# Weight products of a two-layer decoder trunk: three rounded float32r matmuls, or one float32 matmul on the loaded tile

## The reference

```python
for i in range(2):
    mod = silu(c) @ ada_w[i] + ada_b[i]                 # (2048) @ (2048, 12288): read once, a matrix-vector product
    sh1, sc1, g1, sh2, sc2, g2 = split(mod, 6)
    h = x * (1 + sc1) + sh1
    y = s5_mixer(h) if i == 0 else dsa_mixer(h)         # h @ in_w, scan, gelu, @ glu_w  |  h @ in_w, top-64 attention, @ out_w
    x = layer_norm(ALPHA * x + (1 + g1) * y)
    h = x * (1 + sc2) + sh2
    g, u = split(h @ ffn_w_in[i], 2)                    # 2048 -> 2 x 5632
    x = layer_norm(ALPHA * x + (1 + g2) * ((silu(g) * u) @ ffn_w_out[i]))
```

## Time and profile before

| | |
|---|---|
| median of 3 runs | 2871.43 us (2863.91 to 2874.15) |
| span of the profiled execution | 2871.0 us |
| TensorE busy, matmul records | 2560.3 us (89%), 12057 |
| VectorE busy | 2021.9 us (70%) |
| ScalarE busy | 1097.5 us (38%) |
| DMA | 627.74 MB, mean 219 GB/s |
| mean granted TensorE clock | 0.940 |

### The profile page before, as it was taken

The page is one execution under the profiler, slowest core; times in us unless marked ns, Lnnn a source line. Parts: engine busy times, 40 slices in busy tenths (PEclk is TensorE's granted clock), DMA queues, the critical chain, the costliest instruction groups (busy, mean ns, idle before and its releaser), DMA issues.

```text
span 2871.0 us, 35599 instructions
## 1 busy us (share of the span) xinstructions
PE 2560.3 (89%) x12057; PEld 2050.4 (71%) x12057; DVE 2021.9 (70%) x3615; ACT 1097.5 (38%) x1242; POOL 38.5 (1%) x69
## 2 busy tenths in 40 slices
PE   4369668789889999999998999987979999999996
PEld 3357234278768888888886788875868888888885
DVE  6664899958877777677766888678677755455456
ACT  0134532033344434443444344445344434443442
POOL 0000000000000000000000000000000000000000
PEclk8579989889989999999999999977999999999998
DMA  5865313468868888888874788840659856666663
GB/s 195 317 215 192 118 57 124 158 211 306 297 210 285 289 292 292 279 269 286 284 230 161 265 276 273 278 132 26 198 189 306 277 189 193 190 188 193 192 188 126
DMA packets 314890, 627.74 MB, mean 219 GB/s; under 512 B 30816, under 2 KB 31104, under 8 KB 314496
## 3 DMA queue, kind: packets, MB, share of 16 engines
q1 hardware_dynamic: 310272, 611.28, 64.3%
q0 software_dynamic: 4480, 14.68, 1.9%
HBM read 623.77 MB, written 2.10 MB: 218 GB/s over the span
## 4 chain that ended last, share of the span: by engine, by line
PE 71%; DVE 18%; DMA 5%; issue 2%; ACT 2%; SPq 1%; DVEq 0%; POOL 0%; ACTq 0%
PE psB L1495 34%; PE psA L1495 33%; DVE prod L1019 4%; DVE tmp L1024 3%; DVE st L1028 3%; DMA col_raw<-in_ada_w 2%; PE psT L1256 2%; DMA w_raw<-in_s_glu_w 1%; DVE col_acc L828 1%; DVE w_lo L790 1%; DVE ada_acc L802 1%; DMA w_raw<-in_ffn_w_in 1%; PE psM L1273 1%; ACT w_hi L575 0%; ACT st L655 0%
## 5 line engine op out<-in xcount | busy, mean ns | idle before, releaser
L790 DVE TENSOR_TENSOR w_lo<-w_raw,w_hi 128x1024 fp32r<-128x1024 f32 x776 | 947.0, 1224 | 626.9 <-ACT w_hi L575 623.0
L575 ACT ACTIVATE w_hi<-w_raw 128x1024 fp32r<-128x1024 f32 x776 | 819.9, 1060 | 1225.3 <-PE psB L1495 499.9
L1495 PE MATMUL psA<-w_hi,hT_hi 128*128 128x512 f32 (+1 forms) x1216 | 480.6, 395 | 22.4 <-DVE w_lo L790 20.7
L1495 PE MATMUL psB<-w_hi,hT_hi 128*128 128x512 f32 x1184 | 472.6, 399 | 9.0 <-DVE w_lo L790 9.0
L1495 PE MATMUL psA<-w_hi,hT_lo 128*128 128x512 f32 (+1 forms) x1216 | 476.0, 391 | 0.0
L1495 PE MATMUL psA<-w_lo,hT_hi 128*128 128x512 f32 (+1 forms) x1216 | 475.8, 391 | 0.0
L1495 PE MATMUL psB<-w_lo,hT_hi 128*128 128x512 f32 x1184 | 463.9, 392 | 0.0
L1495 PE MATMUL psB<-w_hi,hT_lo 128*128 128x512 f32 x1184 | 463.9, 392 | 0.0
L802 DVE SCALAR_TENSOR_TENSOR ada_acc<-ada_raw,csil,ada_acc 128x512 f32<-128x512 f32 x480 | 359.0, 748 | 13.0 <-DVE ada_acc L802 0.9
L1495 PEld LDWEIGHTS psA<-w_hi,hT_hi 128*128 128x128 f32 x1216 | 232.8, 191 | 72.0 <-DVE w_lo L790 20.3
L1495 PEld LDWEIGHTS psB<-w_hi,hT_hi 128*128 128x128 f32 x1184 | 223.9, 189 | 61.3 <-DVE w_lo L790 12.6
(11 more groups left out here) (272 smaller groups left out, 2314.6 us busy)
## 6 DMA issues: line engine op xcount, KB each, us to landing
w_raw<-in_ffn_w_in SPq DMA_DIRECT2D x352, 512.0 KB, 4.5
ada_raw<-in_ada_w SPq DMA_DIRECT2D x512, 256.0 KB, 4.9
w_raw<-in_ffn_w_out SPq DMA_DIRECT2D x176, 512.0 KB, 4.7
col_raw<-in_ada_w SPq DMA_DIRECT2D x128, 512.0 KB, 4.8
w_raw<-in_dsa_in_w SPq DMA_DIRECT2D x112, 512.0 KB, 4.9
w_raw<-in_s_glu_w SPq DMA_DIRECT2D x64, 512.0 KB, 5.4
w_raw<-in_s_in_w SPq DMA_DIRECT2D x32, 512.0 KB, 5.9
w_raw<-in_dsa_out_w SPq DMA_DIRECT2D x32, 512.0 KB, 4.7
```

Source lines behind the costliest of these rows:

```text
L575: nc.scalar.activation(w_hi[:, n % RING], w_raw[:, n % RING], ACT.Copy).then_inc(w_hi_ready, 1)
L790: V.tensor_tensor(w_lo[:, n % RING], w_raw[:, n % RING], w_hi[:, n % RING].bitcast(F32), ALU.subtract).then_inc(w_lo_ready, 1)
L1495: ins = MM(PS[s][:, t, 0:r.width], a_[:, kt, tok], b_[:, n % RING, kk, 0:r.width], start=kt == 0 and m == 0, stop=k == r.units - 1 and kk ...
```

## The change

The splitting goes, for weights and for activations. TensorE reads `w_raw` and one float32 tile of activations (`hT`, `aT`) and issues one float32 matmul where there were three of float32r. The rings `w_hi` and `w_lo` are no longer written by the stream; the slot of `w_raw` becomes free when TensorE has used it (`w_used`), where before it became free when VectorE had taken the remainder. TensorE waits for the load itself (`w_landed`). The scale-and-shift of ScalarE writes `hT` directly and its semaphore `T_free` lets TensorE begin; so do the gelu, the feed-forward middle and the attention output. `rows_added` is a semaphore for an addition that a removed step used to order.

```diff
-                            sp.wait_ge(w_lo_ready, u + (n - RING + 1 + early))
+                            sp.wait_ge(w_used, u + (n - RING + 1 + early))
...
-            def hi_unit(u, n):
-                act.wait_ge(w_landed[n % RING], u * (16 // RING) + (n // RING + 1) * 16)
-                if not (isinstance(u, int) and u + n < RING):
-                    act.wait_ge(w_used, u + (n - RING + 1))
-                nc.scalar.activation(w_hi[:, n % RING], w_raw[:, n % RING], ACT.Copy).then_inc(w_hi_ready, 1)
...
                     act.wait_ge(T_full, r.hturn + g + 1)
-                    if g >= 2:
-                        act.wait_ge(h_ready, r.h0 + g - 1)
-                    h32 = stg[g % 2][:].rearrange("p a (b t) -> p (a b) t", t=SEQ)
                     for j in range(4):
                         k = 4 * g + j
-                        ins = nc.scalar.activation(h32[:, j], T[:].rearrange("p a (b t) -> p (a b) t", t=SEQ)[:, j],
+                        ins = nc.scalar.activation(hT[:, k], T[:].rearrange("p a (b t) -> p (a b) t", t=SEQ)[:, j],
                                                    ACT.Identity, scale=scol[:, k:k + 1], bias=bcol[:, k:k + 1])
                     ins.then_inc(T_free, 1)
-                    act.wait_ge(T_free, r.hturn + g + 1)
-                    nc.scalar.activation(hT_hi[:, 4 * g:4 * g + 4], h32, ACT.Copy).then_inc(h_hi, 1)
...
-                nc.scalar.activation(y_act[:], y_in[:], ACT.Gelu_apprx_tanh).then_inc(g_ready, 1)
-                act.wait_ge(g_ready, ch + 1)
-                nc.scalar.activation(hT_hi[:, :, ch * TC:(ch + 1) * TC], y_act[:], ACT.Copy).then_inc(g_hi, 1)
+                nc.scalar.activation(hT[:, :, ch * TC:(ch + 1) * TC], y_in[:], ACT.Gelu_apprx_tanh).then_inc(s5_done, 1)
...
-            def lo_unit(u, n):
-                vec.wait_ge(w_hi_ready, u + (n + 1))
-                V.tensor_tensor(w_lo[:, n % RING], w_raw[:, n % RING], w_hi[:, n % RING].bitcast(F32), ALU.subtract
-                                ).then_inc(w_lo_ready, 1)
...
-                        if not (stop and n + AHEAD >= r.per):
-                            lo_unit(u, n + AHEAD)
                         if r.before == "ln" and isinstance(i, int) and i == 0 and n in (3, 6, 9, 12):
+                            vec.wait_ge(T_full, r.hturn + n // 3)
                             affine(r.norm, n // 3 - 1, ALPHA)
...
-                        pe.wait_ge(w_lo_ready, u + (n + 1))
+                        pe.wait_ge(w_landed[n % RING], u * (16 // RING) + (n // RING + 1) * 16)
...
-                                for m, (a_, b_) in enumerate(((hi, w_hi), (hi, w_lo), (lo, w_hi))):
-                                    ins = MM(PS[s][:, t, 0:r.width], a_[:, kt, tok], b_[:, n % RING, kk, 0:r.width],
-                                             start=kt == 0 and m == 0,
-                                             stop=k == r.units - 1 and kk == UK - 1 and m == 2)
+                                ins = MM(PS[s][:, t, 0:r.width], src[:, kt, tok], w_raw[:, n % RING, kk, 0:r.width],
+                                         start=kt == 0, stop=k == r.units - 1 and kk == UK - 1)
```

More of the change, by code:

```diff
@@ L27 @@
 F32 = mybir.dt.float32
-F32R = mybir.dt.float32r
 I32 = mybir.dt.int32
@@ L460, in _ @@
                 if r is glu:
-                    sp.wait_ge(w_lo_ready, glu.unit)
+                    sp.wait_ge(w_used, glu.unit)
                     layer, c0 = column_source(STAGE)
@@ L734, in turned @@
                 if r.kind == "ff" and s == 1:
[L735 removed]
+                    read_T(r, i, 0, aT[:, ds(i * 4, 4)])
                 if r.kind == "ki" and s == 0:
@@ L743, in _ @@
                     s5()
-                    act.wait_ge(y_full, SEQ // TC)
-                    act.wait_ge(g_hi, SEQ // TC)
                 elif r.before == "attention":
                     attention()
[L748 to L752, removed]
                 if r.before in ("x", "ln"):
@@ L756, in _ @@
                     u = r.unit + i * r.per
-                    stop = isinstance(i, int) and i == r.n - 1 and (r is runs[0] or r is runs[-1])
                     last = closing(r, i)
@@ L968, in make_h @@
                 make_scale(r)
-                for g in range(5):
-                    if g < 4 and r.before == "ln":
+                if r.before == "ln":
+                    for g in range(4):
                         normalise(g).then_inc(xn_ready, 1)
-                    if g >= 1:
-                        vec.wait_ge(h_hi, r.h0 + g)
-                        V.tensor_tensor(hT_lo[:, 4 * g - 4:4 * g].rearrange("p a t -> p (a t)"),
-                                        stg[(g - 1) % 2][:].rearrange("p a t -> p (a t)"),
-                                        hT_hi[:, 4 * g - 4:4 * g].rearrange("p a t -> p (a t)").bitcast(F32), ALU.subtract
-                                        ).then_inc(h_ready, 1)
             def affine(norm, chunk, scale, last=None):
@@ L1031, in s5 @@
                             post(ch - 1)
-                        if ch >= 1 and t == 36:
-                            gelu_lo(ch - 1)
                     vec.wait_ge(rec, n)
@@ L1043, in s5 @@
                     ins = V.tensor_tensor(part, part, PS[s][:, :, 0:CW // P], ALU.add)
-                link(ins)
-                gelu_lo(SEQ // TC - 1)
+                ins.then_inc(rows_added, 1)
+                vec.wait_ge(rows_added, 1)
             def rope(r, i, s, heads, half, table):
@@ L1130, in attention @@
                                         ).then_inc(p_ready, 1)
-                    if a % 4 == 3 and a >= 7:
-                        o_lo(a // 4 - 1)
-                o_lo(A // 4 - 1)
             def chain_at(r, i, s):
@@ L1193, in _ @@
                     attention()
-                if r is runs[0] or r is glu:
-                    for n in range(AHEAD):
-                        lo_unit(r.unit, n)
                 if r.before in ("x", "ln"):
@@ L1225, in _ @@
                                 store_chunk(q, q_first)
-                        if n == 3 and last:
-                            turned(*last, last[0].blocks - 1)
                         if r.kind == "glu" and n == r.units + 2:
```

61 lines of the change are left out of this document (19 added, 42 removed).

## The result

| | before | after |
|---|---|---|
| median | 2871.4 us (2863.9 to 2874.2, 4 runs) | 3354.6 us (3347.8 to 3356.7, 4 runs) |
| ratio to before, 95% interval | | 1.168 [1.166, 1.171] |
| span of the profiled execution | 2871.0 us | 3345.9 us |
| TensorE clock granted, mean | 0.940 | 0.957 |

The change makes the kernel 483 us slower. 3356 was forecast.

The account below looks back on a forecast made before the run. TensorE's matmul records times their distance were taken to bound about 2200 of 2871 us. 2871.0 + 546.8 for longer products - 62 for removed waits gave 3355.8, predicted as 3356, range 3325 to 3405.

Parts of the forecast that it names:

- The product, +546.8 us: Weight-product stream: a full unit goes from 2.720 to 3.432 us, 0.712 us more for each of 768 units.
- The gains, 62 us: Places where TensorE stood still for the splitting: 9 + 10 + 30 + 13 us taken off.
- start of "u": At the start of "u", remainders and rounding that TensorE waited for go: 9 us, bounds 3.5 and 13.
- S5 scan: The remainder of L1004 leaves VectorE's scan, 1.14 us three times: 3.4 us gained.
- end of S5 and "glu": At the end of S5 the third unit's load is freed earlier, 6.6 us; "glu" was put at nothing.
- first layer norm's block: First 16 units after the first layer norm: 56.2 us become 47; its share of the norms' 30 us is 9.1.
- attention, third layer norm: Remainders leave VectorE's queue: 8 us before attention and 5 in it, 13 together; 9.0 at the third layer norm.
- What is added: Weight loads: lead falls from up to seven units to three, 10.3 us, against a 4.5 us median load; cost put at nothing.
- The rival of late loads: In each of 32 `ada_w` chunks a load takes 12.0 us and TensorE waits 2.1: 67 us, 3423 in all; chance 0.10.
- The dear record: In the weight-product stream a float32 record takes 440 ns, not 429.1: 3424 us in all; chance 0.05.
- the lower clock: A pure float32 stream is granted less clock, 26 us for each hundredth, three of them 3435; chance 0.03.
- The case of not slower: Every weight product under 0.70 us makes the change pay; at one 0.2267 us record, loads set 2337 us; chance 0.02.

Follow-up runs that it names:

- e1_split_kept: The kernel before with all splitting and its waits kept, only the three float32r products replaced by one float32 product; 3391.3 us, ratio 1.181.
- e9_halves: The changed kernel with each product of 512 columns made as two of 256 with the same stationary tile; 3368.5 us, ratio 1.172.
- e2_three_r: The changed kernel with ScalarE's rounding of each unit put back and three float32r products, VectorE's remainders still out; 2812.8 us, ratio 0.979.
- e4_lead2: The changed kernel with weight loads at most two units ahead of use, where it was three; 3374.3 us, ratio 1.174.
- e3_one_r: The changed kernel with ScalarE's rounding put back and one float32r product, without correction; 2190.8 us, ratio 0.763.

## Why the prediction was right

**What bounds the kernel.** Right: the time was the number of records times their distance. e1_split_kept changes that product alone and has 107% of the whole loss. (The "about 2200 us" of such time was loose: 768 units of 2.720 us are 2089. The sum does not use it.)

**The product, +546.8 us.** The record was put at 0.4291 us from two rows of before; it is 0.4292, so the term becomes 0.713 x 768 = 547.6. The block of 16 units was forecast at 56.7 us and runs from 894.46 to 951.13, 56.67. The decisive step was to price the new matmul by one that already stood in the same stream and to get its digits from a row of back-to-back ones; e9_halves confirms the split into columns and a constant by halving the columns.

The Trainium skill, "FP8 and Floating Point Precision", section "TensorE Precision Notes", lists true float32 as four passes through the array. The traces agree: 858 ns are four times 213.3 and 5. The 131 ns for 512 columns, which the prediction's last rival quotes from the Trainium skill, "TensorE: Matmul & The Clock Gate", section "Back-to-back issue gap", is not seen in any of these kernels; the shortest distance measured is 215.8.

**The gains, 62 us.** By the medians they were 546.8 - 483.2 = 63.6. Between the two traces they were 74 us to the end of the last product. The table sets the prediction's terms beside the stages; "between the traces" is 0.712 us for each full unit of a stage, less what the stage became longer:

| term | predicted | between the traces |
|---|---|---|
| start of "u" | 9 | 10.4 |
| S5 scan | 3.4 | 8.1 |
| end of S5 and "glu" | 6.6 and 0 | 11.6 |
| first layer norm's block | 9.1 | 9.4 |
| layer 0's feed-forward, second layer norm | 11.9 | 13.5 |
| attention, third layer norm | 13 and 9.0 | 21.7 |
| layer 1's feed-forward | 0 | -0.5 |

The norms and attention came out to within 2 us. The excess is in two places, the scan, and the stretch from its end through "glu" (11.6 against 6.6). Of the 11.6, 8.8 were gained by the end of the first eight units, whose successors start at 625.58 before and at 626.83 after. The term counted there the wait for the third unit's load, and not what stood behind the wait in the kernel before: TensorE had been idle for 4.48 us, and its next six units took 19.17 us where 72 records take 16.32, since the granted clock was at its low level again:

```profile
606.00:610.00 4.00, 3.60 (x9) 2.83 (x10) 1.91 (x3) 1.99 (x2) 0.00 (x0) 0.50 1.04 383
```

The other 2.9 us belong to the rest of "glu", which was put at zero, its waits for the splitting set against late loads. The splitting's waits were there before: in the chain of the kernel before, rounding, remainder and the load that they held back follow each other through the second half of the run, as in these rows (start, length, work):

```profile
684.19 1.24 DVE w_lo L790
685.58 5.43 DMA w_raw<-in_s_glu_w
691.03 1.07 ACT w_hi L575
```

The late loads did not come. After the change the chain from the first product of "glu" to the last is TensorE's alone, and the 9.97 us of the earlier trace rows have no successor either:

```profile
596.35 30.48 PE psA L1416 x64
626.83 20.60 PE psB L1416 x48
...
655.15 27.47 PE psA L1416 x64
```

The scan's excess is not the change's. Its length, from the first step to the last copy of `carry`, varies between kernels that have the same steps. Without the remainder of L1004 the six traces give 262.1 (after), 262.8, 267.2, 267.2, 267.6 and 267.7 us, mean 265.8; with it the four give 267.1, 268.0, 270.3 (before) and 273.1, mean 269.6. The 3.8 us between the means fit the 3.4 that were predicted, though each group spreads over 6 us. The pair of before and after happened to lie 8 apart. The two rows that this is read from, of the changed kernel and of e9_halves (durations min/median/max, first and last start):

```profile
L975 DVE TENSOR_TENSOR st<-tmp,st x512: 200/217/779, 311.4 to 573.3; 128x64 f32<-128x64 f32 x171
...
L980 DVE COPY carry<-st x4: 226/227/227, 371.4 to 573.5; 128x128 f32<-128x128 f32 x4
```

```profile
L975 DVE TENSOR_TENSOR st<-tmp,st x512: 200/228/1903, 313.9 to 581.4; 128x64 f32<-128x64 f32 x171
...
L980 DVE COPY carry<-st x4: 226/226/227, 373.9 to 581.6; 128x128 f32<-128x128 f32 x4
```

What makes the scan's length vary stays open.

In one respect the working was too simple. It counted the longer products and the gains as if they were independent. e1_split_kept and e2_three_r show that about 23 us of stalls go with either. The sum was right because the gains were counted once, but from this working the price of one half alone (the splitting's removal in a slow stream) would have been put at 62, and it is 37.

**What was luck.** The terms and the mechanism hold, but 3356 against 3354.6 is closer than the parts are. Term by term the two traces lie 12 us over the forecast of the gains; 8.3 of that vanish in the medians, because of where the two profiled executions lay in their spreads, and 2.3 in the stretch behind the last product, which took that much longer after the change. Two slips of the working are smaller than that: the step from the span to the time was put at 0.4 us and is 1.9 in every run on record, which makes the forecast's own sum 3357.7; and the larger gains add up to 76 us by the bounds given, 14 over 62, where the range took 16.

**What is added.** The load waits were put at nothing, and in the trace they are 0.7 us over all products; the landing times fell as forecast. e4_lead2 shows what stood behind that zero: with a third less of lead it would have been 20 us. The rival of late loads at 67 us was priced with the worst landing in each chunk; in the whole chain of the changed kernel a load into `w_raw` stands once, and TensorE waits those 0.7 us for it:

```profile
2563.76 10.80 DMA w_raw<-in_ffn_w_in
```

**The other rivals.** The dear record (440 ns) and the lower clock fell with the 0.4292 us and the 1.00 in the stream. Of the signs that were named, VectorE's busy time is off, 1065 us against about 1020; the products wait for it 0.4 us in all. The case of not slower needed 0.70 us for a product and got 0.858. Its end of 2337 us, the loads' pace, was itself too high by the rate it assumed: e3_one_r, with one product of 0.2267 us, took 2191.

## What to carry to other kernels

- Price a new instruction by the same shape in the old trace, in the stream where it will stand, and by its distance from the next, not by its busy time. Here two readings of the old trace, the sum over a chunk and the back-to-back row, gave the record's length to 0.1%.
- Fewer instructions and two idle engines are worth little where the third is the bound. 1790 us of work on VectorE and ScalarE went for 37 us (59 or more at the old pace), since it stood beside TensorE.
- A stall that a change removes may also be gone by another part of the same change. Do each half alone before the gain is credited to one of them.
- A row of the chain says what was waited for, and not that the engine stood still. Read the engine's own timeline for the wait, and the granted clock behind it: at the first layer norm of e1_split_kept, 2.1 us of waiting stood in front of 2.0 us more of low clock.

## What was not expected of the hardware

- A float32r matmul of 512 columns takes 226.7 ns from start to start; a bfloat16 one 215.8, and a float32 record with two sweeps of 256 columns 215.8 too. The 11 ns are float32r's own and cost this kernel about 93 us in 2872.
- Loads of 512 KB and 256 KB from one queue reached 371 GB/s at a DMA share of 1.02, though the kernel before had 294 GB/s at 0.88.
- The same chain of small VectorE steps in the S5 scan took 262 to 268 us in six traces in which the same steps stood in it.
- Behind a short wait of TensorE the granted clock was low again: after 2.07 us of waiting in e1_split_kept it was 0.63 (873 to 877 us), after 4.48 us in the kernel before 0.50 (606 to 610 us).
